# Hybrid encoder step: two of three branch products as three-pass split products, fills that run on, and each weight's low part made by two engines

## The reference

```python
xn = _rms_norm(x, P['norm_mix_pre'][l])
cols = jnp.einsum('btd,dc->btc', xn, P['w_in'][l]).astype(jnp.float32)
ca, cb, cc, cg = _split(cols, [A_COLS, B_COLS, C_COLS, N_BRANCH * D_MODEL])
h_a, ... = _mlstm_mixer(ca, ...)      # matrix memory, 4 heads
h_b, ... = _swa_prompt / _swa_sample  # sliding-window attention
h_c, ... = _rwkv_mixer(cc, ...)       # delta-rule state, 8 heads of 64
gates = jax.nn.sigmoid(cg).reshape(Bsz, T, N_BRANCH, D_MODEL)
merged = (gates[:, :, 0] * (h_a @ P['w_branch_a'][l])
          + gates[:, :, 1] * (h_b @ P['w_branch_b'][l])
          + gates[:, :, 2] * (h_c @ P['w_branch_c'][l]))
mix = (merged @ P['w_out'][l]).astype(x.dtype)
x = x + _rms_norm(mix, P['norm_mix_post'][l])
xn = _rms_norm(x, P['norm_ffn_pre'][l])
gate, up = _split(jnp.einsum('btd,df->btf', xn, P['w_ffn_in'][l]), [D_FF, D_FF])
f = jnp.einsum('btf,fd->btd', jax.nn.silu(gate) * up, P['w_ffn_out'][l])
x = x + _rms_norm(f, P['norm_ffn_post'][l])
```

## Time and profile before

| | us |
|---|---|
| median of 3 runs | 2480.55 |
| lowest, highest | 2477.38, 2481.17 |
| profiled execution, device time | 2479.58 |
| its span | 2477.8 |
| mean granted TensorE clock over the span | 0.978 |

### The profile page before, as it was taken

The page is one execution under the profiler, slowest core; times in us unless marked ns, Lnnn a source line. Parts: engine busy times, 40 slices in busy tenths (PEclk is TensorE's granted clock), DMA queues, the critical chain, the costliest instruction groups (busy, mean ns, idle before and its releaser), DMA issues.

```text
span 2477.8 us, 52892 instructions
## 1 busy us (share of the span) xinstructions
PE 2354.7 (95%) x23194; PEld 2218.4 (90%) x23194; DVE 954.7 (39%) x1537; ACT 867.7 (35%) x1671; POOL 723.2 (29%) x566
## 2 busy tenths in 40 slices
PE   7999999998999899999989999999999989999997
PEld 7998888888888899999989988888887889999997
DVE  4426645534323432220073275454443325223102
ACT  4344532221343533222344454222324244323222
POOL 3332211111123244444324222111102133444441
PEclk9999999999899999999999999999999999999998
DMA  5532111111214233233334221111112142223331
GB/s 162 142 79 73 52 27 40 40 28 40 59 45 138 60 91 89 86 90 86 82 106 129 61 73 35 41 40 28 40 40 72 52 140 60 86 86 91 86 92 52
DMA packets 334190, 180.78 MB, mean 73 GB/s; under 512 B 33528, under 2 KB 330648, under 8 KB 332936
## 3 DMA queue, kind: packets, MB, share of 16 engines
q1 hardware_dynamic: 333776, 177.34, 25.6%
q10 hardware_dynamic: 184, 0.05, 0.0%
HBM read 167.98 MB, written 9.38 MB: 72 GB/s over the span
## 4 chain that ended last, share of the span: by engine, by line
PE 82%; DVE 9%; ACT 4%; issue 2%; DMA 1%; SPq 0%; POOL 0%; ACTq 0%; DVEq 0%
PE psum_products L636 73%; PE psum_mixer L636 8%; DMA w_raw<-in_w_in 1%; ACT w_high L1189 1%; ACT L1189 1%; DVE x L1619 1%; DVE squares_ffn L1613 0%; DVE c_in_rate L1699 0%; DVE squares L1586 0%; PE psum_mixer L1004 0%; DVE c_kprime L1779 0%; DVE c_kappa_r L1697 0%; DVE c_in_rate L1752 0%; ACT c_kprime L1189 0%; DVE c_kappa_r L1698 0%
## 5 line engine op out<-in xcount | busy, mean ns | idle before, releaser
L2202 POOL TENSOR_TENSOR w_low<-w_raw,w_high 128x512 fp32r<-128x512 f32 (+1 forms) x542 | 697.9, 1309 | 1617.8 <-ACT w_high L1189 1617.3
L636 PE MATMUL psum_products<-xn_high,w_high 128*128 128x272 f32 (+1 forms) x3424 | 738.0, 297 | 27.4 <-DVE xn_low L1568 12.3
L636 PE MATMUL psum_products<-xn_high,w_low 128*128 128x272 f32 (+1 forms) x3424 | 711.8, 289 | 0.0
L636 PE MATMUL psum_products<-xn_low,w_high 128*128 128x272 f32 (+1 forms) x3424 | 709.1, 289 | 0.0
L636 PEld LDWEIGHTS psum_products<-xn_high,w_high 128*128 128x128 f32 x3424 | 544.1, 190 | 48.3 <-issue 20.1
L636 PEld LDWEIGHTS psum_products<-xn_low,w_high 128*128 128x128 f32 x3424 | 543.5, 190 | 0.0
L636 PEld LDWEIGHTS psum_products<-xn_high,w_low 128*128 128x128 f32 x3424 | 540.1, 190 | 0.0
L1189 ACT ACTIVATE w_high<-w_raw 128x512 fp32r<-128x512 f32 (+1 forms) x542 | 308.0, 617 | 215.2 <-PE psum_products L636 134.1
L636 PE MATMUL psum_products<-hidden_high,w_high 128*128 128x272 f32 x704 | 145.9, 288 | 0.0
L636 PE MATMUL psum_products<-hidden_high,w_low 128*128 128x272 f32 x704 | 145.7, 288 | 0.0
L636 PE MATMUL psum_products<-hidden_low,w_high 128*128 128x272 f32 x704 | 145.1, 288 | 0.0
(11 more groups left out here) (361 smaller groups left out, 2877.3 us busy)
## 6 DMA issues: line engine op xcount, KB each, us to landing
w_raw<-in_w_in SPq DMA_DIRECT2D x112, 512.0 KB, 4.0
w_raw<-in_w_ffn_in SPq DMA_DIRECT2D x88, 512.0 KB, 3.8
w_raw<-in_w_ffn_out SPq DMA_DIRECT2D x32, 512.0 KB, 3.8
w_raw<-in_w_out SPq DMA_DIRECT2D x16, 512.0 KB, 4.0
w_raw<-in_w_ffn_out SPq DMA_DIRECT2D x16, 384.0 KB, 3.3
x_kept<-x SPq DMA_DIRECT2D x2, 2176.0 KB, 7.5
x<-x_kept SPq DMA_DIRECT2D x2, 2176.0 KB, 9.7
w_raw<-in_w_in SPq DMA_DIRECT2D x16, 256.0 KB, 3.7
```

The source lines that it names most:

```text
L636: return pe.matmul(out, lhsT, rhs, start=start, stop=stop, skip_group_check=True)
L2202: low_ready.inc(pool.tensor_tensor(wl[:, n % NSPLIT, ks_], wraw[:, slot, ks_], wh[:, n % NSPLIT, ks_].bitcast(F32), ALU.subtract))
```

## The change

Branches a and c become split units of 4 blocks with three passes; branch b stays as it is. Their activations are split too: `a_out_split` is a new item ahead of the first gate (ScalarE `a_out_high`, VectorE `a_out_low`), and `c_finish` splits each piece of branch c when it is made. `merged` is split block by block behind each branch c unit. When the next unit is finished, `fill` may go on into the unit behind it. `c_chain` gets `fill(1)` ahead of the products that need `neg_z`, and `fill(3)` behind. The tanh of the next group moves from `c_prep` to `c_level` 3 of the group before. GpSimd makes the first half of each low part, VectorE the second, at the beginning of the next item in its order (`low_rest`).

```diff
         plan += second
-        plan += [("gate", l) + GATES[0], ("c_shift_out", l)]
+        plan += [("a_out_split", l), ("gate", l) + GATES[0], ("c_shift_out", l)]
         c = []
...
          "ffn_gate": "dve", "ffn_up": "dve", "ffn_out": "act"}
-UNSPLIT = {"branch"}
+def unsplit(s):
+    return s[0] == "branch" and s[2] == 1
 EARLY = (0, 1, 2, 16, 3, 4)
...
     y_tok = place("y_tokens", [P, 5, D], arena)
+    a_low = place("a_out_low", [P, 4, T], acols_at + 4 * AQ * T, F32R)
+    a_high_at = ((a_rb_at + 4 * (2 * 1024 + 2 * 512) + 31) // 32 * 32, (rest + 4 * 4 * T + 31) // 32 * 32)
+    assert a_high_at[0] + 4 * 2 * T <= bh_at and a_high_at[1] + 4 * 2 * T <= acols_at + 4 * AQ * T
+    a_high_two = [place(f"a_out_high{i}", [P, 2, T], at_, F32R) for i, at_ in enumerate(a_high_at)]
+    class Blocks:
+        def __getitem__(self, key):
+            return a_high_two[key[1] // 2][key[0], key[1] % 2]
+    a_high = Blocks()
...
             else:
-                eng.wait_ge(low_ready.sem, 2 * low_no[n] - 1 + half)
+                eng.wait_ge(low_ready.sem, low_no[n])
+                if half:
+                    eng.wait_ge(low_rest_ready.sem, low_no[n])
         def half_blocks(s):
...
                     l, b, m = s[1:]
-                    rhs = [(acols[:, AQ + k, :], bh[:, k, :], cc[:, k, :])[b] for k in range(4)]
-                    gemm(s, rhs=rhs, nk=4, steps=steps)
+                    if b == 0:
+                        gemm(s, rh=a_high, rl=a_low, nk=4, steps=steps)
+                    elif b == 1:
+                        gemm(s, rhs=[bh[:, k, :] for k in range(4)], nk=4, steps=steps)
+                    else:
+                        gemm(s, rh=c_high, rl=c_low, nk=4, steps=steps)
                 else:
...
                          wait_k=s in steps_of, steps=steps)
+            def fillable(s):
+                return (s[0] in ("cols_b", "cols_c", "gate") or (s[0] == "cols_a" and 12 <= s[2] < 16)
+                        or (s[0] == "branch" and s[2] < 2 and s[3] > 0))
             def fill(steps):
-                if unit_at[0] < len(units):
-                    s = units[unit_at[0]]
-                    if (s[0] in ("cols_b", "cols_c", "gate") or (s[0] == "cols_a" and 12 <= s[2] < 16)
-                            or (s[0] == "branch" and s[3] > 0)):
-                        product(s, steps)
+                u = unit_at[0]
+                while steps > 0 and u < len(units) and u < unit_at[0] + 2 and fillable(units[u]):
+                    s = units[u]
+                    there = done_k.get(s, 0)
+                    product(s, steps)
+                    steps -= done_k[s] - there
+                    u += 1
             steps_of = set()
...
                 bank[1].filled(last, "dve")
+                fill(1)
                 bank[1].claim(pe)
...
                 bank[3].filled(last, "act", ("c_y", l, g, c))
-                fill(4)
+                fill(3)
             def c_state_out(l, g):
...
                 step(fn(stats[0:1, 60:61], stats[0:1, 60:61], ACT.Copy), flow("shift_rows"))
+            def tanh_ahead(l, g):
+                n, at, nch, L = c_group(g)
+                step(fn(tanh_w[:, 0:n], cc[0:64, 12, at:at + n], ACT.Tanh), flow("c_tanh_w"))
             def c_prep(l, g):
...
                     act.wait_ge(flow("b_stored").sem, 96 * (l + 1))
-                step(fn(tanh_w[:, 0:n], cc[0:64, 12, at:at + n], ACT.Tanh), flow("c_tanh_w"))
+                    tanh_ahead(l, 0)
                 flow("c_kk_raw").wait_next(act, "act")
...
                 step(fn(y_rn[:], y_rn[:], ACT.Exp, scale=-0.5), flow("c_gn_r"))
+            def c_finish(l, f):
+                flow("c_out").wait_next(act, "act")
+                step(fn(c_high[:, f, 0:T], cc[:, f, 0:T], ACT.Copy), flow("c_out_high"))
+            def a_out_high(l):
+                flow("a_out").wait_next(act, "act")
+                for h in range(4):
+                    step(fn(a_high[:, h], acols[:, AQ + h, :], ACT.Copy), flow("a_out_high"))
             def cols_a(s):
...
                 step(fn(halves(dst), pair_view(pair), ACT.Tanh, scale=0.5), emptied["act"])
+            def merge_high(k):
+                flow("merged").wait_next(act, "act")
+                xh_ready.inc(fn(xh[:, k, :], merged[:, k, :], ACT.Copy, scale=0.5))
             def merge_split(l):
-                for k in range(KD):
-                    flow("merged").wait_next(act, "act")
-                    xh_ready.inc(fn(xh[:, k, :], merged[:, k, :], ACT.Copy, scale=0.5))
+                merge_high(KD - 1)
             for s in plan:
...
                                  bank[half].empty["act"])
-                elif kind in ("branch", "c_finish", "c_scale", "c_gram", "c_level", "a_rows_put", "a_rows_get", "a_scale",
+                elif kind == "branch" and s[2] == 2 and s[3] > 0:
+                    merge_high(s[3] - 1)
+                elif kind == "c_level":
+                    if s[3] == 3 and s[2] + 1 < GROUPS:
+                        tanh_ahead(s[1], s[2] + 1)
+                elif kind in ("branch", "c_scale", "c_gram", "a_rows_put", "a_rows_get", "a_scale",
                               "a_out", "bias_put", "bias_get", "a_state_put", "b_put", "c_shift_put", "c_state_put"):
...
                 return tiles[s][0]
+            def low_rest(n):
+                s = split_units[n]
+                ks_ = half_blocks(s)[1]
+                dve.wait_ge(high_ready.sem, 2 * low_no[n])
+                step(tt(wl[:, n % NSPLIT, ks_], wraw[:, unit_no[s] % NRAW, ks_], wh[:, n % NSPLIT, ks_].bitcast(F32), SUB),
+                     low_rest_ready)
             def load_x():
...
+                        if k < 3:
+                            low_rest(k)
                 else:
...
                 step(dve.tensor_copy(stats[0:1, 61:62], stats[0:1, 61:62]), flow("c_dev"))
+            def c_out_low(f):
+                flow("c_out_high").wait_next(dve, "dve")
+                step(tt(c_low[:, f, 0:T], cc[:, f, 0:T], c_high[:, f, 0:T].bitcast(F32), SUB), flow("c_h") if f == 3 else None)
             def c_finish(l, f):
...
                 step(tt(cc[:, f, TP:T], d[:, TP + 1:CW], mp[bk + 1][:, TP + 1 - Y_CUT:CW - Y_CUT], MUL), bank[bk + 1].empty["dve"])
+                step(dve.tensor_copy(stats[0:1, 61:62], stats[0:1, 61:62]), flow("c_out"))
+                if f:
+                    c_out_low(f - 1)
                 if f == 3:
-                    step(dve.tensor_copy(stats[0:1, 61:62], stats[0:1, 61:62]), flow("c_h"))
+                    c_out_low(3)
             def a_rows(l):
...
                 if g == GROUPS - 1:
-                    step(dve.tensor_copy(stats[0:1, 61:62], stats[0:1, 61:62]), flow("a_h"))
+                    step(dve.tensor_copy(stats[0:1, 61:62], stats[0:1, 61:62]), flow("a_out"))
+            def a_out_low(l):
+                for h in range(4):
+                    flow("a_out_high").wait_next(dve, "dve")
+                    step(tt(a_low[:, h, :], acols[:, AQ + h, :], a_high[:, h].bitcast(F32), SUB), flow("a_h") if h == 3 else None)
             def b_values(l):
...
                     step(tt(merged[:, m, :], merged[:, m, :], dst, ADD), flow("merged") if b == 2 else None)
+                if b == 2 and m:
+                    merge_low(l, m - 1)
+            def merge_low(l, k):
+                dve.wait_ge(xh_ready.sem, split_base(l, 2) + k + 1)
+                step(stt(out=xl[:, k, :], in0=merged[:, k, :], scalar=0.5, in1=xh[:, k, :].bitcast(F32),
+                         op0=MUL, op1=SUB), xl_ready)
             def hidden_low(j):
...
                 step(tt(hid_l[:, j, :], ffn_p[:, j % 2, :], hid_h[:, j, :].bitcast(F32), SUB), flow("hidden"))
+            split_last = ()
             for s in plan:
                 kind, l = s[0], s[1] if len(s) > 1 else 0
+                for n in split_last:
+                    low_rest(n)
+                split_last = ()
+                if ahead.get(s) and kind != "norm_post":
+                    split_last = ahead[s]
                 if kind == "load_x":
...
                 elif kind == "merge_split":
-                    for k in range(KD):
-                        dve.wait_ge(xh_ready.sem, split_base(l, 2) + k + 1)
-                        step(stt(out=xl[:, k, :], in0=merged[:, k, :], scalar=0.5, in1=xh[:, k, :].bitcast(F32),
-                                 op0=MUL, op1=SUB), xl_ready)
+                    merge_low(l, KD - 1)
                 elif kind == "ffn_gate":
...
                 slot = unit_no[s] % NRAW
-                for half, ks_ in enumerate(half_blocks(s)):
-                    pool.wait_ge(high_ready.sem, 2 * low_no[n] - 1 + half)
-                    low_ready.inc(pool.tensor_tensor(wl[:, n % NSPLIT, ks_], wraw[:, slot, ks_],
-                                                     wh[:, n % NSPLIT, ks_].bitcast(F32), ALU.subtract))
+                ks_ = half_blocks(s)[0]
+                pool.wait_ge(high_ready.sem, 2 * low_no[n] - 1)
```

(10 more changed lines are left out.)

5 lines of the change are left out of this document (3 added, 2 removed).

## The result

The changed kernel takes 2547.23 us (median; 2545.83 to 2553.39) beside 2480.01 us for the kernel before on the same chip: ratio 1.0287, 95% interval 1.0272 to 1.0302. The forecast was 2462 us with a range up to 2492; it is slower by 67 us instead of faster by 17.

What follows compares the result with a forecast made beforehand. TensorE, busy 95% of the span, was taken as the bound. Gains of 52.6 us less losses of 39.4, rounded to 13 to 20 net, taken as 17, gave 2462 us from 2479.6; the 8-in-10 range was 2428 to 2492.

Steps and rivals of the forecast that it cites:

- The work is not the price; the place is.: VectorE's second halves: some 250 operations, 175 us of work in 1500 idle, cost by standing ahead of the mixers' items.
- 39.4 us of losses: All predicted losses: 1.4 at branch c's start, 13 attention, 12 variance, 11 RWKV levels, 2 first projections and mLSTM chunks.
- Attention, -13: VectorE's halves delay score reads: 7 us at two chunks a layer, 6 at attention's start; loss 13, ends 4 and 30.
- Variance, -12: VectorE's halves delay the squares 2.6 us at two of four places, partly at one; loss 12, ends 3 and 18.
- The clock, put at nothing: Clock time lost behind the new waits was not in the sum, which was rounded to 13 to 20 us net.
- RWKV levels, -11 (0 to 40): VectorE's halves in the RWKV stage: 0.35 us for each of 31 units, 11 us lost; ends 0 and 40.
- I put it at nothing: Run-on fills waiting for the next unit's weights: no cost assumed, as raw blocks lie ready; the fills' gain was 5 us.
- Branch a, +5: Split products of branch a, 16 units between RWKV mixer steps: 5 us gained, the middle of 0 to 10.6.
- branch c and merge as it comes: Branch c's split products gain 10.6 us, splitting merged early gains 11, late splits at branch c's start lose 1.4.
- chain fill with tanh: RWKV stage: the fill inside the state chain gains 10 of 11.7 us of waits, the early tanh 7 of 11.5.
- Rival 2: VectorE's queue becomes the bound of the mixers: 69 us of loss against 53 of gain, 2496 us; chance 0.20.
- The sign that I had set for it: For the rival of VectorE's queue: VectorE's releases head TensorE's list of waits with over 60 us.

Runs made afterwards that it cites:

- e1: The changed kernel with both halves of each low part written by GpSimd again: 2466.71 us, ratio 0.9951.
- e3: The kernel before with only the second half of each low part moved to VectorE: 2571.33 us, ratio 1.0371.
- e14: e5 with GpSimd writing only 16 elements of each low part half of branch a's weights: 2446.21 us, ratio 0.9876.
- e7: The kernel before with only branch c in split passes and merged split as it comes: 2458.74 us, ratio 0.9934.
- e6: The kernel before plus, on VectorE, only the wait for ScalarE's second high half and a one-element copy at each new place: 2520.93 us, ratio 1.0177.
- e11: e3 with GpSimd's half of each low part cut to 16 elements: 2523.15 us, ratio 1.0194.
- e5: The changed kernel with low parts whole on GpSimd and fills that stop at the next unit: 2455.26 us, ratio 0.9909.
- e8: e7 plus the fill inside the state chain and the early tanh, branch a in plain fp32: 2437.75 us, ratio 0.9844.

## Why the prediction was wrong

- **"The work is not the price; the place is."** Right in that each new operation costs by what stands behind it, wrong as a sum. This is the first failed step. Of the 39.4 us of losses, 38 belonged to this part (13 + 12 + 11 + 2); it costs 83 (e1), 92 alone (e3: 32 + 27 + 26 + 7). The mechanism is the one named, and the single places that I worked out have the right size: 1.30 us for the new operation, 1.8 us more at the earlier trace rows, 2.6 us at the earlier trace rows. What was mis-sized is the number of places, and what follows each was left out.
- **Attention, -13.** Measured 32 us in e3; the changed kernel's stage is 38 longer, and 5 of them stay in e1. Over the stage in the first layer TensorE's idle time (length less its busy time, in the windows above) goes from 5.0 to 17.4 us, and the other 5.2 us of the 17.6 are busy time at a mean granted clock of 0.93 for 0.99. Half of that idle time, 8.8 us, lies in the first 51 us, where five of the new operations stand: waits of 4.22 us for a_cols and 3.33 for b_scores_even. I had put 3 us a layer there, for four.
- **Variance, -12.** Measured 27, in e3 and in the changed kernel. I counted the 2.6 us at two of four places and in part at one; it is there at two, and 5.2 us at a third, where two new operations stand. That is 10.4 us a layer, and the slower clock behind each wait (1.19 us become 2.19) makes it 13.4.
- **The clock, put at nothing.** I had left it to a rounding: "clock time lost behind the new waits is not in it". It was 96 us more at the lower level, by the estimate above about 42 us of the time.
- **RWKV levels, -11 (0 to 40).** Measured 26 in e3. In the changed kernel the stage is 17 us longer in two layers in all, with its gains and the run-on fills' cost in it.
- **"I put it at nothing"**, the danger of a run-on fill. That is the second failed step: raw blocks lie ready, but the split does not. Instead of +5, -10 to -16 with branch a split, -32 without.
- **Branch a, +5.** Measured -16. The sum had the bound "0 to 10.6" from TensorE's side and held the weight splits to be beside products; the earlier trace rows had shown what a low part does to a VectorE operation, and I used it for the new operations alone. About half of the price is that, by e14; the other half stays open.
- **Right:** branch c and merge as it comes (10.6 + 11 - 1.4 = +20.2 forecast, +16 measured by e7, in whose trace the stage is 19.5 us shorter), and chain fill with tanh (+17, +22 measured).
- **The whole:** put together by the runs, -16 (branch c, merge) - 22 (chain fill, tanh) + 16 (branch a) + 10 (run-on fills) + 83 (VectorE's halves) = +71. Rival 2, that VectorE's queue becomes the bound of the mixers, was the right one. Even its 69 us of loss were low, and of the 53 us of gains that it was set against the runs leave 38, less the 16 and 10 that two of the parts cost. The sign that I had set for it, VectorE's releases with over 60 us of TensorE's waits, could not have told: they sum to 78 us before and 92 after. The parts were measured against different versions and do not simply add: the run-on fills cost 16 us beside VectorE's halves, 10 without them and 32 with branch a unsplit.

## What to carry to other kernels

On an in-order engine, an operation that waits for another engine costs by how long it holds up what is queued behind it, its wait as well as its own length: here the bare wait cost 44 us, with 38 us of new work on an engine that was busy 39% of the span, and the wait with 1.235 us behind it cost 92. Before putting such work on the engine with the most idle time, list for each place what stands next in its queue and who waits for that. If the critical engine waits for it, leave the work on an engine behind which nothing waits. A fill that borrows from the next unit needs everything of that unit ready, its split included. And TensorE's new waits have to be priced with the half clock behind them: in the changed kernel's trace waits as short as 2.0 us (207.18) were followed by a stretch at the lower level, though one of 3.15 us (650.4) was not.

## What was not expected of the hardware

- A wait alone, on an engine that is busy 39% of the span, costs 44 us of 2478 (e6: 268 waits with a copy of 0.14 us behind each).
- An operation of about 1.23 us on VectorE costs the same whether it is 1024 elements alone (+93 us) or 512 beside GpSimd (+92 us).
- Where one operation of each engine meets, VectorE's is the one that is stretched: the 128x512 shape takes 697 ns in e11 and 1251 in e3, and GpSimd's 1320 in e3 against 1327 before. GpSimd's has begun first there (267.28 against 267.82). Where VectorE has several such operations in a row, GpSimd's are stretched too: 1.60 and 1.71 us in the stretch of e5 above, 1.27 and 1.26 in that of e8.
- GpSimd's low parts cost VectorE's other operations 60 us of busy time in all (935 us in e6, 875 in e11, where GpSimd writes next to nothing).
